# A 64-byte strip in front of the two split-weight buffers of a two-block fp32 transformer kernel

## The chip, the cores and the metric

The kernel runs on one core of one Trainium2 chip. The metric is the device time of one execution in microseconds. Below, the time before is the median of three runs; one more execution was taken by the hardware profiler, and every duration in the text comes from that one.

## The reference, cut to what matters

Two transformer blocks in fp32 on 256 tokens of width 2048. The first has an adaptive modulation, a wide input projection, stick-breaking and sparse attention, an output projection and a gated feed-forward network with a short convolution. The second block is run twice (two layers) with an input projection, small latent projections, three kinds of attention and an output projection. What fills the time are the products of a 256-token activation with a weight matrix from HBM:

```python
proj = h @ w_in[l]                       # 2048 x 5456
x = x + g1 * (merged @ w_out[l])         # 2048 x 2048
u = h @ w_up                             # 2048 x 11008
... @ w_down                             # 5504 x 2048
proj = jnp.einsum('bsd,dn->bsn', h, w_in[l])      # 2048 x 6726, twice
x = x + jnp.einsum('bsm,md->bsd', mixed, w_out[l])  # 2048 x 2048, twice
```

## The kernel before, in words

**Split products.** Each fp32 operand of a large product is split in two: a high part rounded to the type `fp32r` (which TensorE takes in one pass), and a low part, the rest. A product is three terms: high by high, low by high, high by low. The activation's parts are `HH` and `HLO` (line 109: 16 blocks of 128 rows by 256 tokens, each block 1024 bytes per partition), the weight's parts are `WHI` and `WLO` (line 116: four slots of 1024 columns each, 4096 bytes per partition).

**The stream of weights.** SyncE loads raw fp32 weights from HBM into `RAWT` (line 115, four slots of 2048 columns). For every half slot ScalarE writes the high part to `WHI` (`hi`, line 294), VectorE subtracts and writes the low part to `WLO` (`lo`, line 302), and TensorE runs the three terms (`three_terms`, lines 311 and 312, and `up_pe`, lines 1405, 1406 and 1410). Semaphores tie them: ScalarE may overwrite a slot when TensorE is past the product four half slots back, VectorE waits for ScalarE, TensorE waits for both. The order is written by hand.

**Two forms of matmul.** In the *row form* (line 312) an activation block of 128 tokens is loaded into the array as the stationary operand, and the weights stream through as the moving operand: 512 columns in the output projections and the down projection, 512, 496, 448, 416, 388 or 386 in the input projections. The moving operand then lies in `WHI` or `WLO`. In the *column form* (line 311, and 1405, 1406, 1410 for the up projection) 128 weight columns are stationary and the activation streams, 256 tokens: the moving operand lies in `HH` or `HLO`, the stationary in `WHI` or `WLO`. The latent products of block two take the activation from `LATHI` and `LATLO` (lines 110 to 112, names for places inside `BIG`) in either form; there the row form has 384 columns. Lines 877 to 879 are the row form at the end of an output projection, and 388 and 413 the modulation's share, interleaved with block one.

**Where things lie.** `sb` (line 103) asks for buffers one after the other, and the allocator puts them in that order, each start rounded up to 32 bytes. Per partition:

- `X`, `HH`, `HLO` and `BIG` start on multiples of 128 bytes (even multiples of 64).
- `BIG` has 13452 columns, 53808 bytes, which is 420 times 128 and 48 bytes more. `RAWT` therefore starts 64 bytes past a multiple of 128, an odd multiple of 64.
- `RAWT`, `WHI`, `WLO`, `AD`, `WK` and `KX` are multiples of 128 bytes long, so `WHI`, `WLO`, `AD`, `WK`, `KX` and `CST` all start on odd multiples of 64 too. `PV`, `MODC`, `BADA` and `SM` follow behind.
- `LATHI` starts 12608 bytes into `BIG` and `LATLO` 39488: both odd multiples of 64.

Inside a slot of `WHI` the two blocks of rows lie one behind the other (line 535: `o = (q % HL) * GR + k * n`, and the same in the other products), so with 512, 448 or 416 columns (2048, 1792, 1664 bytes) both blocks start with the parity of the buffer. With 496 columns (1984 bytes, an odd multiple of 64) the two blocks have opposite parity.

Of the kernel before, what the change touches and what calls it, by code (L numbers as in the profile page):

```python
# [93 lines left out]
def build_program(nc, x, c, positions, w_ada, b_ada, norm1_g, w_in, sb_norm_g, dsa_norm_g, w_out, norm2_g,  # L94
# [7 lines left out]
    with ctx:  # L102
        def sb(name, cols, dt=F32):
            return ctx.enter_context(nc.sbuf_tensor(name, [P, cols], dt))
# [8 lines left out]
            pass  # L113
        BIG = sb("BIG", 2 * W2)
        RAWT = sb("RAWT", RAW * 2 * GR)
        WHI, WLO = sb("WHI", HL * GR, F32R), sb("WLO", HL * GR, F32R)
        AD = sb("AD", 5 * 1024)
        WK = sb("WK", 3072)
# [159 lines left out]
        def raw_slot(gs):  # L278
            return RAWT[:, (gs % RAW) * 2 * GR:(gs % RAW + 1) * 2 * GR]

# [2383 lines left out]
```

How the kernel before makes its waits and increments, by code:

```python
        def ge(eng, sem, v):  # L172
            if isinstance(v, int) and v <= 0:
                return
            eng.wait_ge(sem, v)
# [7 lines left out]
            def __call__(self, ins):  # L184
                self.n += 1
                ins.then_inc(self.sem, 1)
                self.eng.wait_ge(self.sem, self.n)
# [99 lines left out]
        def hi(act, gs, reg, per_slot, j, size):  # L287
            q = 2 * gs + j
            if j == 0:
                act.wait_ge(raw_in[gs % RAW], reg * per_slot + uses[gs])
            ge(act, S("mm_done"), reg * 2 + (q - 3))
            r = raw_slot(gs)[:, j * size:(j + 1) * size]
            act.activation(WHI[:, (q % HL) * GR:(q % HL) * GR + size], r, ACT.Copy).then_inc(S("hi_done"), 1)
# [1 line left out]
        def lo(dve, gs, reg, j, size):  # L296
            q = 2 * gs + j
            dve.wait_ge(S("hi_done"), reg * 2 + (q + 1))
            r = raw_slot(gs)[:, j * size:(j + 1) * size]
            h = WHI[:, (q % HL) * GR:(q % HL) * GR + size]
            dve.tensor_tensor(WLO[:, (q % HL) * GR:(q % HL) * GR + size], r, h.bitcast(F32), ALU.subtract)\
               .then_inc(S("lo_done"), 1)
# [1 line left out]
        def three_terms(pe, parts, hi_at, lo_at, first, last):  # L305
# [6 lines left out]
                    pe.matmul(o, feat, weight, start=start, stop=stop)  # L312
            pe.wait_ge(S("hi_done"), hi_at)
            seen = set()
# [2 lines left out]
                seen.add(part[0])  # L318
                term(part, 1)
            pe.wait_ge(S("lo_done"), lo_at)
            left = [part[0] for part in parts]
```

## Time and profile before

| | |
|---|---|
| median of 3 runs | 2121.39 us (2120.06 to 2126.27) |
| the profiled execution's own time | 2119.28 us |
| its span, first to last instruction | 2117.4 us |
| granted TensorE clock, mean over the span | 0.987 |
| TensorE busy | 97% of the span, 13976 matmuls |
| VectorE, ScalarE, GpSimd busy | 66%, 48%, 6% |
| HBM read | 458.62 MB |

A busy row of TensorE counts a matmul from its start to its modelled end. Matmuls overlap in the pipeline, so a record is longer than the distance between two starts. That distance is called the pitch below.

### The profile page before, as it was taken

To read this page: it belongs to the slowest core of one execution; us is meant where nothing else is said; L and a number is where in the kernel's file an instruction comes from. 1 tells how busy PE (TensorE), PEld (TensorE's weight loads), DVE (VectorE), ACT (ScalarE), POOL (GpSimd) and SP (SyncE) were. 2 spreads that over 40 slices of the span, in tenths; PEclk is the share of its full clock that TensorE was granted. 3 is DMA by queue.
4 is the path that set the end of the run, shared out by engine and by line. 5 is a ranking of instruction groups with operands and counts; after the bars stand their busy time and mean duration, and the time that the engine had idled before them with its cause. 6 is when DMAs were issued, how large, how long until landed. Compare 5 with 4: busy or idle time off the path is not lost.

```text
span 2117.4 us, 33915 instructions
## 1 busy us (share of the span) xinstructions
PE 2055.6 (97%) x13976; PEld 1863.1 (88%) x13976; DVE 1404.7 (66%) x2153; ACT 1008.2 (48%) x1490; POOL 130.1 (6%) x113
## 2 busy tenths in 40 slices
PE   4999999998999999999999999999999999999997
PEld 1678998787999999998888899999988999999986
DVE  2358999886767667666567576556666756566665
ACT  2234445634554444454545455444564544445653
POOL 0000000012000000000011021000010110000100
PEclk6999999999999999999999999999999999999999
DMA  9998799593777777656655546545555556445553
GB/s 361 382 356 312 240 385 331 204 345 124 246 243 243 233 235 240 195 173 240 191 177 200 183 155 188 202 149 161 162 191 184 164 160 219 161 157 163 178 194 119
DMA packets 267317, 462.97 MB, mean 219 GB/s; under 512 B 21526, under 2 KB 160028, under 8 KB 266652
## 3 DMA queue, kind: packets, MB, share of 16 engines
q1 hardware_dynamic: 265832, 459.66, 64.2%
q8 instruction: 111, 1.82, 0.4%
q10 hardware_dynamic: 1332, 1.14, 0.2%
q14 instruction: 42, 0.34, 0.0%
HBM read 458.62 MB, written 2.13 MB: 218 GB/s over the span
## 4 chain that ended last, share of the span: by engine, by line
PE 86%; DVE 6%; DMA 3%; issue 2%; ACT 2%; ACTq 1%; POOL 0%; SPq 0%; DVEq 0%
PE PS L312 37%; PE PS L311 20%; PE PS L1405 7%; PE PS L1410 7%; PE PS L1406 7%; DVE WLO L302 2%; PE PS L1248 2%; DMA BIG<-w_ada 1%; ACT WHI L294 1%; PE PS L413 1%; DMA X<-x 1%; PE PS L1262 1%; DVE WK L1087 1%; DVE BIG L1733 1%; PE PS L1077 0%
## 5 line engine op out<-in xcount | busy, mean ns | idle before, releaser
L302 DVE TENSOR_TENSOR WLO<-RAWT,WHI 128x1024 fp32r<-128x1024 f32 (+7 forms) x694 | 829.8, 1202 | 401.0 <-ACT WHI L294 400.0
L294 ACT ACTIVATE WHI<-RAWT 128x1024 fp32r<-128x1024 f32 (+7 forms) x694 | 694.1, 1015 | 359.9 <-PE PS L1410 195.4
L312 PE MATMUL PS<-WHI,HH 128*128 128x512 f32 (+5 forms) x1296 | 503.3, 388 | 7.1 <-POOL HLO L1096 3.2
L312 PE MATMUL PS<-WHI,HLO 128*128 128x512 f32 (+5 forms) x1296 | 494.5, 382 | 0.0
L312 PE MATMUL PS<-WLO,HH 128*128 128x512 f32 (+5 forms) x1296 | 337.5, 382 | 1.3 <-DVE WLO L302 1.3
L1405 PE MATMUL PS<-HH,WHI 128*128 128x256 f32 x1376 | 327.1, 279 | 5.9 <-POOL HLO L1096 5.9
L1406 PE MATMUL PS<-HLO,WHI 128*128 128x256 f32 x1376 | 326.1, 278 | 0.0
L311 PE MATMUL PS<-HH,WHI 128*128 128x256 f32 x1280 | 312.0, 285 | 0.0
L311 PE MATMUL PS<-HLO,WHI 128*128 128x256 f32 x1280 | 303.2, 278 | 0.0
L312 PEld LDWEIGHTS PS<-WHI,HH 128*128 128x128 f32 x1296 | 244.4, 189 | 54.1 <-issue 7.2
L312 PEld LDWEIGHTS PS<-WLO,HH 128*128 128x128 f32 x1296 | 243.5, 189 | 43.1 <-DVE WLO L302 2.0
L312 PEld LDWEIGHTS PS<-WHI,HLO 128*128 128x128 f32 x1296 | 244.7, 189 | 39.1 <-issue 0.2
L1405 PEld LDWEIGHTS PS<-HH,WHI 128*128 128x128 f32 x1376 | 259.3, 188 | 7.3 <-POOL HLO L1096 7.3
L1406 PEld LDWEIGHTS PS<-HLO,WHI 128*128 128x128 f32 x1376 | 259.6, 189 | 0.0
L311 PEld LDWEIGHTS PS<-HH,WHI 128*128 128x128 f32 x1280 | 241.2, 188 | 6.4 <-issue 6.0
L311 PEld LDWEIGHTS PS<-HLO,WHI 128*128 128x128 f32 x1280 | 241.3, 189 | 0.4
L1410 PE MATMUL PS<-HH,WLO 128*128 128x256 f32 x1376 | 188.1, 279 | 0.0
L311 PE MATMUL PS<-HH,WLO 128*128 128x256 f32 x1280 | 174.4, 279 | 1.6 <-DVE WLO L302 1.6
L1410 PEld LDWEIGHTS PS<-HH,WLO 128*128 128x128 f32 x1376 | 172.1, 189 | 0.0
L311 PEld LDWEIGHTS PS<-HH,WLO 128*128 128x128 f32 x1280 | 159.2, 188 | 2.3 <-DVE WLO L302 2.2
L388 DVE SCALAR_TENSOR_TENSOR AD<-AD,SM 128x1024 f32<-128x1024 f32 x75 | 96.9, 1292 | 4.2 <-DMA AD<-w_ada 3.5
L814 ACT ACTIVATE HH<-BIG 128x256 fp32r<-128x256 f32 x102 | 42.1, 414 | 107.4 <-PE PS L312 106.7
(309 smaller groups left out, 1627.7 us busy)
## 6 DMA issues: line engine op xcount, KB each, us to landing
RAWT<-w_in SPq DMA_DIRECT2D x96, 1024.0 KB, 5.2
RAWT<-w_up SPq DMA_DIRECT2D x168, 512.0 KB, 4.9
AD<-w_ada SPq DMA_DIRECT2D x152, 512.0 KB, 6.3
RAWT<-w_out SPq DMA_DIRECT2D x96, 512.0 KB, 4.8
RAWT<-w_down SPq DMA_DIRECT2D x86, 512.0 KB, 4.6
BIG<-w_ada SPq DMA_DIRECT2D x40, 512.0 KB, 12.1
RAWT<-w_in SPq DMA_DIRECT2D x16, 832.0 KB, 4.6
RAWT<-w_in SPq DMA_DIRECT2D x16, 512.0 KB, 4.3
```

What stands on the lines that cost most here:

```text
L294: act.activation(WHI[:, (q % HL) * GR:(q % HL) * GR + size], r, ACT.Copy).then_inc(S("hi_done"), 1)
L302: dve.tensor_tensor(WLO[:, (q % HL) * GR:(q % HL) * GR + size], r, h.bitcast(F32), ALU.subtract)\
L311: return pe.matmul(o, weight, feat, start=start, stop=stop) if stationary else \
L312: pe.matmul(o, feat, weight, start=start, stop=stop)
L388: dve.scalar_tensor_tensor(acc, w, CS[:, kt:kt + 1], acc, ALU.mult, ALU.add)\
L413: mm = pe.matmul(PS[32 * j:32 * j + 32, 7, 0:T], col, w[:, j * T:(j + 1) * T], start=False, stop=kt == KT - 1)
L814: eng.activation(HHv[:, r, :], src(kt), ACT.Copy).then_inc(S("st_hi"), 1)
L1087: op = eng.tensor_scalar(f[:, j * T:(j + 1) * T], pb[:, j * T:(j + 1) * T], scale(kt), None if bias is None else bias(kt), ALU.mult, ALU.b ...
L1248: mm = eng.matmul(blk(scores(both[k], m + k), hf), l, r, start=z == 0, stop=z == len(prs[0]) - 1)
L1405: pe.matmul(o, WHI[:, wt[k, t]], HHv[:, kt, :], start=kt == 0 and t % 2 == 0, stop=False)
L1406: pe.matmul(o, WHI[:, wt[k, t]], HLv[:, kt, :], start=False, stop=False)
L1410: mm = pe.matmul(ffn_tile(par, t), WLO[:, wt[k, t]], HHv[:, kt, :], start=False, stop=kt == KT - 1 and t % 2 == 1)
```

## The change

An unused buffer of 16 fp32 columns, 64 bytes per partition, is allocated between `RAWT` and `WHI`. No instruction is added, removed or moved. `X`, `HH`, `HLO`, `BIG` (with `LATHI` and `LATLO`) and `RAWT` stay where they are; every buffer behind moves up by 64 bytes, so that `WHI`, `WLO`, `AD`, `WK`, `KX` and `CST` start on multiples of 128 bytes. `PV`, `MODC`, `BADA` and `SM` move as well.

```diff
         BIG = sb("BIG", 2 * W2)
         RAWT = sb("RAWT", RAW * 2 * GR)
+        sb("SHIFT", 16)
         WHI, WLO = sb("WHI", HL * GR, F32R), sb("WLO", HL * GR, F32R)
         AD = sb("AD", 5 * 1024)
```

## Rows read from the trace of the kernel before

**Rows 1.** The page: span, TensorE's busy share, and the chain that ended last.

```profile
span 2117.4 us, 33915 instructions
PE 2055.6 (97%) x13976; PEld 1863.1 (88%) x13976; DVE 1404.7 (66%) x2153; ACT 1008.2 (48%) x1490; POOL 130.1 (6%) x113
...
PE 86%; DVE 6%; DMA 3%; issue 2%; ACT 2%; ACTq 1%; POOL 0%; SPq 0%; DVEq 0%
```

**Rows 2.** Waits of TensorE: waiter, what it waited for: total us, times, longest.

```profile
PE PS L413 <- DMA AD<-w_ada: 10.1, 6, 4.4
PE PS L413 <- DMA BIG<-w_ada: 9.8, 10, 2.8
...
PE PS L312 <- DVE WLO L302: 1.3, 2, 0.7
```

**Rows 3.** Steady stretches: bounds, length, PE busy (matmuls), clock, DMA share, GB/s.

```profile
520.00:700.00 180.00, 180.00 (x1591) 1.00 0.77 249
710.00:885.00 175.00, 175.00 (x1488) 1.00 0.72 231
...
985.00:1105.00 120.00, 120.00 (x526) 1.00 0.63 204
...
156.00:167.50 11.50, 11.50 (x59) 1.00 1.01 378
142.00:152.00 10.00, 10.00 (x46) 1.00 0.78 266
1233.00:1245.50 12.50, 12.50 (x68) 1.00 0.55 170
```

**Rows 4.** Groups by line and shape: count, busy us, mean ns, idle before.

```profile
L312 PE MATMUL PS<-WHI,HH 128*128 128x512 f32 x880 | 349.4, 397 | 3.8 <-DVE HLO L820 2.0 <-ACT WHI L294 1.2 <-issue 0.6
...
L1405 PE MATMUL PS<-HH,WHI 128*128 128x256 f32 x1376 | 327.1, 279 | 5.9 <-POOL HLO L1096 5.9
...
L311 PE MATMUL PS<-HH,WHI 128*128 128x256 f32 x1280 | 312.0, 285 | 0.0
...
L312 PE MATMUL PS<-WHI,HH 128*128 128x416 f32 x128 | 45.7, 357 | 0.0
L312 PE MATMUL PS<-WHI,HH 128*128 128x496 f32 x96 | 40.2, 419 | 3.2 <-POOL HLO L1096 3.2
L312 PE MATMUL PS<-WHI,HH 128*128 128x448 f32 x64 | 23.8, 372 | 0.0
...
L877 PE MATMUL PS<-WHI,HH 128*128 128x512 f32 x32 | 12.5, 390 | 0.0
...
L312 PE MATMUL PS<-WHI,LATHI 128*128 128x384 f32 x16 | 5.4, 335 | 0.0
```

**Rows 5.** Pieces of the chain that ended last: start us, us, what.

```profile
1297.12 8.62 PE PS L311 x72
1305.74 4.17 PE PS L312 x24
...
1335.70 2.75 PE PS L311 x24
...
1338.67 2.83 PE PS L311 x24
```

**Rows 6.** Groups on VectorE in 412 to 446, block one's output projection.

```profile
L302 DVE TENSOR_TENSOR WLO<-RAWT,WHI 128x1024 fp32r<-128x1024 f32 x12 | 16.5, 1372 | 0.0
L388 DVE SCALAR_TENSOR_TENSOR BIG<-AD,SM,BIG 128x1024 f32<-128x1024 f32 x6 | 7.7, 1276 | 0.0
L388 DVE SCALAR_TENSOR_TENSOR AD<-AD,SM 128x1024 f32<-128x1024 f32 x5 | 7.4, 1482 | 0.0
```

**Rows 7.** Busy times in the same stretch; the columns PE, PEld, DVE, ACT, POOL.

```profile
412.00:446.00 34.00, 34.00 (x156) 28.10 (x155) 32.92 (x33) 14.95 (x18) 7.05 (x4) 1.00 0.92 342
```

**Rows 8.** Groups in 985 to 1105, the down projection.

```profile
L302 DVE TENSOR_TENSOR WLO<-RAWT,WHI 128x1024 fp32r<-128x1024 f32 x45 | 56.2, 1249 | 20.4 <-ACT WHI L294 20.4
L294 ACT ACTIVATE WHI<-RAWT 128x1024 fp32r<-128x1024 f32 x46 | 48.0, 1044 | 0.0
...
L820 DVE TENSOR_TENSOR HLO<-BIG,HH 128x256 fp32r<-128x256 f32 x44 | 19.5, 443 | 22.3 <-ACT HH L814 22.3
```

## The prediction

> **What bounds the kernel now.** The page first: TensorE is busy for 97% of a span of 2117.4 us, and 86% of the chain that ended last is its matmuls [rows 1]. Then its waits: the longest totals are 10.1 and 9.8 us, for transfers of the modulation's weights, and for the low parts of the weights it waited 1.3 us [rows 2]. In the long stretches it has no gap at all, at a granted clock of 1.00, that is 2.4 GHz [rows 3]. So the time is the number of matmuls times their pitch, and a layout that changes the pitch changes the time.
>
> **The pitch, and how it comes out of a row.** A stretch of length L counts every record that touches it, so pitch = (L + one record) / count. The records last some 390 ns with 512 columns and 279 with 256 [rows 4]. Then [rows 3]:
>
> - Column form, moving `HH` (even start): (180000 + 279) / 1591 = 113.3 ns in one stretch and (175000 + 279) / 1488 = 117.8 ns in another, the same instructions. In cycles of 2.4 GHz that is 256 + 16 and 256 + 27: two modes, each of which lasts as long as a stretch does. Short pieces show the same two: 2.75 us for 24 is 114.6, 2.83 us is 117.9 [rows 5].
> - Row form, 512 columns, moving `WHI` (odd start): 120392 / 526 = 228.9 ns, 512 + 37 cycles. 448 columns: 11872 / 59 = 201 ns, 448 + 35. 416 columns: 12857 / 68 = 189 ns, 416 + 38.
> - Latent products, moving `LATHI` (odd start): 8.62 us for 72 is 119.7 ns, 256 + 31; moving `WHI` over a stationary `LATHI`: 4.17 us for 24 is 173.8 ns, 384 + 33 [rows 5].
>
> What is to be seen: the surplus over one cycle per column doesn't grow from 256 to 448 columns, so it is a toll per matmul. It is 31 to 38 wherever the moving operand starts on an odd multiple of 64 bytes, and 16 or 27 where it starts on an even one. At equal width (256) the odd start costs 119.7 against 113.3, that is 6.4 ns, about 16 cycles, as many as 64 bytes of fp32 columns. The stationary operand doesn't sort the rows: it is odd for `HH` by `WHI`, odd for `LATHI` by `WHI`, even for `WHI` by `HH`.
>
> **The change part by part.** No instruction comes or goes. Four things move.
>
> 1. *Moving operand in `WHI` or `WLO`, odd to even.* I take off the 6.4 ns seen at equal width. The 512-column group counts 880, with its two sister terms 2640 matmuls, and lines 877 to 879 add 3 x 32 = 96; 416 columns: 3 x 128 = 384; 384 columns: 3 x 16 = 48; 448: 3 x 64 = 192 [rows 4]. Not all of them pay. In block one's output projection, 412 to 446 standing for 306 to 480 us, VectorE is busy 32.9 of 34.0 us beside a gapless TensorE, with modulation work of 1276 and 1482 ns apiece between its splits [rows 6, 7]: if TensorE speeds up, `WLO` is late next. That is 576 matmuls, which I count at nothing. The 448-column products run at a DMA share of 1.01 and 378 GB/s [rows 3]: nothing either. The 496-column ones change which half is odd, not how many: nothing. There remain 2064 + 96 + 384 + 48 = 2592, times 6.4 = 16.6 us, rounded to 17. In the down projection the cover is ample: per 12 matmuls (2.75 us) VectorE needs 1249 + 443 ns and ScalarE 1044 plus a split of that size, DMA moves 204 GB/s [rows 3, 8]; with 2.67 us they still fit.
>    Ends: if the toll falls to the even group's 16 cycles, 512 columns go to 220.0 ns, 8.9 less, and the sum is 2592 x 8.9 = 23 us. If it falls to 27, 224.6, 4.3 less, 11 us.
> 2. *Stationary operand in `WHI` or `WLO`, odd to even, under a moving `HH`.* 3 x (1376 + 1280) = 7968 matmuls [rows 4]. No row shows this pair of starts. By the chain's pieces about 3,000 of them now run at 117.8, half of these in one stretch around 710 to 885. Why a stretch takes one mode isn't to be seen, so I leave the mix: nothing. Ends: all in the fast mode, 3000 x 4.4 = 13 us less; all in the slow mode, 5000 x 4.4 = 22 us more.
> 3. *What ScalarE writes and VectorE reads and writes.* 694 splits on either engine. VectorE takes 1249 ns with an odd `WLO` [rows 8]; there is no even counterpart of that shape, so I take no change. They hide behind 2.75 us of matmuls; a price shows only in 306 to 480 us, where 48 splits at 5% of 1372 ns would be 3 us either way [rows 6].
> 4. *Buffers behind (`AD`, `WK`, `CST`, `SM`).* The same instructions on addresses 64 bytes up, a few per cent of TensorE's time: nothing, ends within those of point 3.
>
> Sum: 17 us less. The profiled execution's span would be 2117.4 - 17 = 2100; its own time, 2119.3, is 2.1 below the median, 2121.4, from which I subtract: **2104 us**, 0.8% less. A measurement of this kernel can tell about 0.3%, 6 us, from no change.
>
> **A rule weighed against the rows.** The granted pitch of 512 moving columns is 228.9 ns, of 256 it is 113.3 to 117.8 [rows 3]. The Trainium skill ("TensorE: Matmul & The Clock Gate", Back-to-back issue gap) gives the gap of warm matmuls as N/2.4 plus some 2.5 ns, 216 ns at 512 columns, and knows no toll for a start address. If the shift took the whole toll away, its figure would give 2592 x 12.9 = 33 us less for point 1, 2088 us. No row here comes within 10 cycles of it, so it enters nothing.
>
> **The rivals.**
>
> *Nothing happens: the start isn't the cause.* `LATHI` differs from `HH` in more than parity (short products, other distance to `WHI`), and the toll of the row form may belong to a weight stream that two engines write meanwhile. For: the 496-column products, half of which start even already, have (10000 + 397) / 46 = 226 ns, 496 + 46, the highest toll of all [rows 3]. Against: the toll is 31 to 33 both with `LATHI` moving, which nobody writes then, and with `WHI` moving over it [rows 5]. Time: 2121, give or take 5. The Trainium skill sides with this rival ("SBUF — State Buffer", Specifications): lines of 16 bytes, of which either start is a whole multiple. The forecast coupled with all column-form matmuls in the slow mode (17 less, 22 more) ends here as well. Chance 0.18.
>
> *Slower: the loads collide with the streams.* The load of the next stationary operand starts with the current matmul, so two streams read at once. Now an even `HH` streams over an odd `WHI`; after the change both start even. The one column-form case of equal parity in the trace is `LATHI` by `WHI`, both odd, and it is the slowest, 119.7 [rows 5]. If equal parity is the cause, the 7968 column-form matmuls go from a mean of (4968 x 113.3 + 3000 x 117.8) / 7968 = 115.0 to 119.7: 37 us more. The row form would lose at most its surplus over 33 cycles, 1.7 ns x 2592 = 4 us. Time: 2121 + 33 = 2154. It decides from the point where the column form's mean pitch passes 115.0 + 17000 / 7968 = 117.1; there it has eaten the gain. Against: `WHI` over `HH` is unequal now and pays 35 to 38. Chance 0.14.
>
> *More than forecast.* The mode of 117.8 comes of the odd stationary start, and with it gone all run at 113.3, and the row form at 16 cycles of toll: 13 + 23 = 36 us less, 2085. For: every matmul with an even moving and an even stationary start is unseen. Chance 0.13.
>
> *The change doesn't do what it says.* The strip could end up elsewhere, or unallocated; the starts follow from the order and sizes of the buffers, and the strip keeps its place. Below 0.02, counted with the first rival.
>
> **How the numbers follow.** Forecast 0.55, by itself 2092 to 2116: the row form's 11 to 23, the mix some 5 either way. With nothing 0.18, slower 0.14, more 0.13. The range leaves out 0.06 below, where the third case is complete, and 0.12 above, most of the slower case: 2083 to 2128. Faster by over 0.3%: the forecast but for 0.02, and the third case, 0.66. Slower by over 0.3%: the slower case and 0.02 of the first: 0.16. Within 0.3%: 0.18.
>
> **What would show it.** In 985 to 1105 us the 512-column matmuls at 222.5 ns (some 541 in 120 us for 526) confirm point 1; 220.0 is the upper end, 228.9 the first rival. The column form in 520 to 885 us tells point 2: 113.3 or 117.8, and 119.7 or more is the slower rival. The latent products (72 in 8.62 us) should stay if the moving start alone counts. The 496-column ones should stay at 226. VectorE waited for by TensorE between 306 and 480 us shows the share I count at nothing. It is wrong if pitches fall that I don't name, or if the pitch falls as said and the time doesn't, through waits for `WLO`.

## The result, and the profile after

The changed kernel takes 2151.1 us in the median (2150.3 to 2151.9, 4 runs) beside 2121.8 us for the kernel before: ratio 1.0144, 95% interval 1.0128 to 1.0159. It is slower by 29 us (27 to 34 by the ratio's interval), where 17 us less, 2104 us, was forecast, and lies outside the range of 2083 to 2128. The rival "the loads collide with the streams" had 2154 us and a chance of 0.14.

The page of the changed kernel, against [rows 1]; its lines are numbered one higher from line 116 on:

```profile
span 2148.9 us, 33915 instructions
PE 2093.3 (97%) x13976; PEld 1892.2 (88%) x13976; DVE 1405.0 (65%) x2153; ACT 1009.7 (47%) x1490; POOL 129.9 (6%) x113
...
PE 88%; DVE 6%; issue 2%; ACT 2%; DMA 2%; ACTq 1%; POOL 0%; SPq 0%; DVEq 0%
```

The same 13976 matmuls keep TensorE busy for 37.7 us more (2093.3 against 2055.6), while the other engines' busy times stay within 1.5 us. TensorE's idle time falls by 6.2 us (span less busy: 55.6 against 61.8), and 37.7 - 6.2 is the span's 31.5. So TensorE doesn't wait more; the matmuls themselves are further apart.

Steady stretches, as in [rows 3] (bounds, length, PE busy and matmuls, clock, DMA share, GB/s):

```profile
520.00:700.00 180.00, 180.00 (x1502) 1.00 0.74 237
710.00:885.00 175.00, 175.00 (x1478) 1.00 0.72 231
...
1000.00:1120.00 120.00, 120.00 (x516) 1.00 0.63 204
156.00:167.50 11.50, 11.50 (x59) 1.00 0.99 383
142.00:152.00 10.00, 10.00 (x46) 1.00 0.98 358
```

By the prediction's formula the column form now has (180000 + 283) / 1502 = 120.0 and (175000 + 283) / 1478 = 118.6 ns where it had 113.3 and 117.8. The row form with 512 columns has (120000 + 395) / 516 = 233.3 where it had 228.9. Pieces of the chain, against [rows 5]:

```profile
1316.40 8.18 PE PS L312 x72
1324.58 4.16 PE PS L313 x24
```

The latent products, whose moving operand did not move, went the other way: 8.18 us for 72 is 113.6 ns, before 119.7. That is the line that decides against "the moving start counts alone".

In the down projection the splits take what they took [rows 8]:

```profile
L303 DVE TENSOR_TENSOR WLO<-RAWT,WHI 128x1024 fp32r<-128x1024 f32 x44 | 53.9, 1225 | 20.6 <-ACT WHI L295 20.6
...
L295 ACT ACTIVATE WHI<-RAWT 128x1024 fp32r<-128x1024 f32 x45 | 47.0, 1044 | 0.0
```

Taken over the whole trace from the distances between starts, with the gaps of waits left out, the column form's mean rises from 115.3 to 119.0 ns (7770 distances: 29 us), the 512-column row form's from 229.1 to 232.8 (2660: 10 us), the latent column form's falls from 119.7 to 114.9 (214: 1 us). That is 38 us, against the 37.7 that the page shows. Of the other widths, 448 columns rise from 200.6 to 203.7 ns, and 416 stay (188.1 and 188.4).

### The profile page after: what moved, and what is told of

Read it like the earlier page. It is cut to its first block, busy times and chain, and to the rows that moved or that the text cites. A ratio compares the mean times of both kernels' runs of the same rounds, so it can differ in the third digit from the quotient of the medians.

```text
span 2148.9 us, 33915 instructions
## 1 busy us (share of the span) xinstructions
PE 2093.3 (97%) x13976; PEld 1892.2 (88%) x13976; DVE 1405.0 (65%) x2153; ACT 1009.7 (47%) x1490; POOL 129.9 (6%) x113
## 4 chain that ended last, share of the span: by engine, by line
PE 88%; DVE 6%; issue 2%; ACT 2%; DMA 2%; ACTq 1%; POOL 0%; SPq 0%; DVEq 0%
PE PS L313 38%; PE PS L312 20%; PE PS L1406 7%; PE PS L1411 7%; PE PS L1407 7%; DVE WLO L303 2%; PE PS L1249 2%; PE PS L414 1%; ACT WHI L295 1%; DMA X<-x 1%; PE PS L1263 1%; DVE WK L1088 1%; DVE BIG L1734 1%; DMA BIG<-w_ada 1%; PE PS L1078 0%
## 5 line engine op out<-in xcount | busy, mean ns | idle before, releaser
L1406 PE MATMUL PS<-HH,WHI 128*128 128x256 f32 x1376 | 338.3, 284 | 4.7 <-POOL HLO L1097 4.7
L1407 PE MATMUL PS<-HLO,WHI 128*128 128x256 f32 x1376 | 337.1, 283 | 0.0
L312 PE MATMUL PS<-HH,WHI 128*128 128x256 f32 x1280 | 319.5, 288 | 0.0
L312 PE MATMUL PS<-HLO,WHI 128*128 128x256 f32 x1280 | 311.2, 282 | 0.0
L1411 PE MATMUL PS<-HH,WLO 128*128 128x256 f32 x1376 | 193.0, 282 | 0.0
L312 PE MATMUL PS<-HH,WLO 128*128 128x256 f32 x1280 | 178.2, 282 | 0.2 <-DVE WLO L303 0.2
L1411 PEld LDWEIGHTS PS<-HH,WLO 128*128 128x128 f32 x1376 | 176.3, 189 | 0.0
L312 PEld LDWEIGHTS PS<-HH,WLO 128*128 128x128 f32 x1280 | 163.0, 188 | 0.4 <-DVE WLO L303 0.4
```

The source lines that it names most:

```text
L312: return pe.matmul(o, weight, feat, start=start, stop=stop) if stationary else \
L1406: pe.matmul(o, WHI[:, wt[k, t]], HHv[:, kt, :], start=kt == 0 and t % 2 == 0, stop=False)
L1407: pe.matmul(o, WHI[:, wt[k, t]], HLv[:, kt, :], start=False, stop=False)
L1411: mm = pe.matmul(ffn_tile(par, t), WLO[:, wt[k, t]], HHv[:, kt, :], start=False, stop=kt == KT - 1 and t % 2 == 1)
```

## The experiments

Two theories were tested one after the other. The first, which the expectations of the first four experiments (e1 to e4) state, was equal parity: a matmul is slow when both operands start on odd, or both on even, multiples of 64 bytes. e1 refuted it, and from e5 on the theory is that the distance between the places of the two operands counts. Call D the start of `WHI` less the start of the activation's buffer, modulo 256 bytes. It is 64 for `HH` and 0 for `LATHI` before the change, 128 and 64 after it. (`HH` and `HLO`, `WHI` and `WLO`, and the blocks inside them lie multiples of 256 bytes apart, but for products of 496, 416, 388 or 386 columns. At 416 the two blocks have D = 64 and 192 before and 128 and 0 after, at 448 both have 64 and then 128.) Pitches below are means of start distances in steady stretches. In the stretches looked at, a steady column form on a given D takes one of at most two values.

**Where does the strip have to stand?** Four kernels, each the kernel before with one edit:

```diff
 e1_strip128:     RAWT = sb("RAWT", RAW * 2 * GR)
+        sb("SHIFT", 32)
 e2_all_moved:    X = sb("X", 2 * D)
+        sb("SHIFT", 16)
 e3_behind_wlo:   WHI, WLO = sb("WHI", HL * GR, F32R), sb("WLO", HL * GR, F32R)
+        sb("SHIFT", 16)
 e4_between:      WHI = sb("WHI", HL * GR, F32R)
+        sb("SHIFT", 16)
+        WLO = sb("WLO", HL * GR, F32R)
```

> Strip of 128 bytes in front of WHI instead of 64: WHI and WLO are odd again, HH stays even. Theory (equal parity of the moving and the stationary start, as an odd or even multiple of 64 bytes, makes the load collide with the stream): parities are unequal again, so the time returns to that of before, 2121 us within 6, the column form to 113.3 or 117.8 ns, LATHI by WHI back to 119.7. Rival (the distance counts in more than its parity, or any move away from the old place hurts): a time of its own, 2130 or more, or a pitch that neither kernel has.

2144.3 us, ratio 1.0105 (1.008 to 1.013). Parity is refuted as the rule: `WHI` is odd again and the time does not come back. Stretches of this kernel, with the columns of [rows 3]: the column form runs at 117.8 in nearly every stretch (113.3 in two short ones), the row form at 233.3, and the latent products (D now 128) at 118.6:

```profile
520.00:690.00 170.00, 170.00 (x1446) 1.00 0.76 246
720.00:885.00 165.00, 165.00 (x1403) 1.00 0.71 232
1015.00:1105.00 90.00, 90.00 (x388) 1.00 0.61 191
```

(170283 / 1446 = 117.8, 165283 / 1403 = 117.8, 90396 / 388 = 233.0; one record more or less in the count is 0.6 ns, and the start distances themselves give 233.3.) The rival "more than its parity" stands.

> The 64-byte strip stands in front of HH, so HH, HLO, BIG, RAWT, WHI and WLO all move by 64 bytes: WHI and WLO are even as in the changed kernel, but HH is odd, so that the parities are unequal. Theory (equal parity collides): 2121 us within 6. Rival (an even start of WHI and WLO is itself the cause, by its own streams or by what ScalarE and VectorE write there): 2151 us.

2116.3 us, ratio 0.998 (0.9963 to 0.9996). `WHI` lies as in the changed kernel, and the cost is gone. The place of the weights by itself doesn't matter; the column form has 113.3 and 117.8 again, the row form 228.9, and `LATHI`, moved along, 119.7.

> The strip stands behind WLO: WHI and WLO stay, and only AD, WK, KX, CST and the small buffers behind move by 64 bytes. Theory (equal parity of HH and WHI): 2121 us within 6. Rival (the 29 us come from the other buffers that the change moved, AD, WK and CST): up to 2151 us.

2119.0 us, ratio 0.9983 (0.9965 to 1.000). The buffers behind cost nothing.

> The strip stands between WHI and WLO: WHI stays odd, WLO is even. One of three terms, high by low, has equal parity with HH. Theory (it is a matter of the two starts of one matmul and its neighbour): about a third of the 29 us, 2128 to 2134 us, with the pitch of the WLO term raised alone or with a neighbour of it. Rival (both weight buffers must be even, or VectorE's reading and writing of unequal starts matters): 2121 or 2151 us.

2124.1 us, ratio 1.001 (0.9995 to 1.0025), less than the 2128 to 2134 expected. The pitches rise by about their third in the row form (229.1 to 230.6) but by only a sixth in the column form (115.3 to 115.9 against 119.0). Its steady stretches, with the columns of [rows 3]:

```profile
520.00:690.00 170.00, 170.00 (x1473) 1.00 0.75 243
720.00:885.00 165.00, 165.00 (x1431) 1.00 0.73 236
```

That is 115.6 and 115.5 ns, and (2 x 113.3 + 120.0) / 3 is 115.5. So the thirds come out if the two unmoved terms take the fast mode everywhere, also in 720 to 885 us, where the kernel before ran at 117.8. Why they take it with the third term at another distance isn't shown. The time moves less than the pitches: TensorE's busy time is 8.5 us above before (2064.1 against 2055.6), the profiled span only 2.8 (2120.2 against 2117.4), as its idle time falls.

**How does the cost go with the distance?** Buffers that exist anyway serve as strips, as there is too little room for empty ones; `MODC` and `BADA` no longer stand at their old place where they appear here:

```diff
 e5_strip32:      RAWT = ...
+        sb("SHIFT", 8)
 e6_384_64:       RAWT = ...
+        MODC = sb("MODC", 96)
+        sb("SHIFT", 16)
 e7_768:          RAWT = ...
+        MODC = sb("MODC", 96)
+        BADA = sb("BADA", 96)
 e8_384_96:       RAWT = ...
+        MODC = sb("MODC", 96)
+        sb("SHIFT", 24)
```

> Strip of 32 bytes in front of WHI. What counts is taken to be the distance from HH to WHI and WLO; 64 bytes more cost 29 us, 128 bytes more 23 us. Theory (the distance modulo 256 bytes, in steps of 64): a start inside a step behaves as a mixture, 2121 to 2151 us, with a column-form pitch between 115.3 and 119.0 ns. Rival (any start off a multiple of 64 bytes costs one more access per stream): slower than both, over 2155 us.

2149.4 us, 1.0119 (1.0059 to 1.0178). D is 96: column form 117.3 or 118.7, row form 233.4. Inside the theory's range, but at its upper end, and the row form is above both neighbours, so steps of 64 bytes are too coarse a picture. The rival's 2155 us or more isn't reached.

> MODC (384 bytes) and a strip of 64 bytes stand in front of WHI, so the distance from HH grows by 448 bytes. Modulo 256 it is then a whole multiple, the case of LATHI by WHI in the kernel before (119.7 ns in the column form, 173.6 ns for 384 columns in the row form). Theory (distance modulo 256 bytes): column form at 119.7 to 120, row form near 229 ns, so 4.5 x 7770 = 35 us more, 2150 to 2158 us. Rival (parity modulo 128 bytes, with a detail that the 128-byte strip upset): as the changed kernel, column form 119.0 and row form 232.8 ns. Rival (only the distance modulo 512 or more counts): pitches not seen yet.

2146.6 us, 1.0115 (1.0087 to 1.0144). D is 0 for `HH`, and its column form is now at 120.0 everywhere, the value that `LATHI` had. The latent products, at 192, take 113.5 (8.17 us for 72). The row form falls to 227.3, below before, which makes the total 3 us less than the least I expected.

> MODC and BADA (768 bytes together) stand in front of WHI: the distance from HH grows by three times 256 bytes. Theory (distance modulo 256 bytes): as before, 2121 us within 6, column form at 113.3 or 117.8 ns, row form 229.1, LATHI by WHI 119.7. Rival (modulo 512 bytes or a larger power of two): 768 is half of 512 away from a multiple, so pitches and time differ from before, by 10 us or more.

2119.9 us, 0.9991 (0.9964 to 1.0018). Three times 256 bytes change no pitch. This settles the period of 256 bytes against 512 and larger powers of two; e1 had excluded 128.

> MODC (384 bytes) and a strip of 96 bytes in front of WHI: the distance from HH is 32 bytes past a multiple of 256, half a step below that of the kernel before. Theory (distance modulo 256): column form between that of a whole multiple (119.7) and that of before (115.3), 2121 to 2156 us. Rival (half a step suits the load and the stream better): column form at 113.3 throughout, some 15 us below before, 2106 us.

2150.8 us, 1.0128 (1.0068 to 1.0188). D is 32: column form 118.3, row form 233.3. Half way between the two places is no better place.

> The 64-byte strip stands in front of RAWT, so RAWT moves along with WHI and WLO; HH, HLO and BIG stay. Theory (distance from HH to WHI): as the changed kernel, 2151 us within 6, with column form 119.0 and row form 232.8 ns. Rival (the distance from RAWT to WHI and WLO, over which ScalarE and VectorE split the weights): 2121 us.

```diff
         BIG = sb("BIG", 2 * W2)
+        sb("SHIFT", 16)
         RAWT = sb("RAWT", RAW * 2 * GR)
```

2148.9 us, 1.0131 (1.0103 to 1.0159), column form 118.7, row form 232.8: the changed kernel again, with `RAWT` moving along. So the distance from `RAWT` to `WHI` and `WLO`, over which the weights are split, isn't the cause.

> All as in the kernel before, but LATHI and LATLO lie 64 bytes further into BIG, so that their distance to WHI leaves the whole multiple of 256 bytes. Theory: the latent products in the column form go from 119.7 to 113.3 ns, 432 matmuls, 2.6 us less in all, 2116 to 2119 us; everything else keeps its pitch. Rival (the short products are slow for another reason): 119.7 ns and the time of before.

```diff
-LATENT, KVB = (3152, 9872), W2 - 1536
+LATENT, KVB = (3168, 9888), W2 - 1536
```

Pieces of the chain of waits in this kernel, as in [rows 5]:

```profile
1296.50 8.16 PE PS L311 x72
1304.67 4.19 PE PS L312 x24
```

2118.9 us, 0.9994 (0.9981 to 1.0008): too small for the timing, but plain in the pitch. D of the latent products is 192 instead of 0, and 72 take 8.16 us instead of 8.62, with nothing else moved.

**The cost by itself.**

```python
def col(i, d):
    k, t = i % 8, i // 2 % 8
    return PS[:, k % 4, 0:T], WHI[:, d // 4 + t * P:d // 4 + (t + 1) * P], HH[:, k * T:(k + 1) * T]
...
for i in range(96): pe.matmul(*col(i, 64), start=True, stop=True)
```

> The disputed cost by itself. This kernel leaves out the whole computation: it loads one stretch of weights, makes an HH and a WHI of them, and then runs nothing but blocks of 96 matmuls, each block at another distance from HH to WHI (0 to 320 bytes in the column form, 0 to 256 in the row form), with the other engines idle. Its output is a copy of a piece of input. Theory (the load of the next stationary operand and the stream of the moving one collide by their distance modulo 256 bytes): the same pitches as in the full kernels, column form 120 ns at 0 and 256, 113.3 or 117.8 at 64, 192 and 320, 118.7 to 120 at 128; row form lower at 0 and 64 (227, 229) than at 128 and 192 (233). Rival (the collision is with what ScalarE, VectorE or the transfers write): one pitch at all distances.

Groups by line of this kernel, one block of 96 matmuls each: the row form at D = 0, then the column form at D = 128, 256, 160, 192, 64 and 320 (count, busy us of the block, mean ns of a record):

```profile
L169 PE MATMUL PS<-WHI,HH 128*128 128x512 f32 x96 | 22.0, 390 | 0.0
...
L157 PE MATMUL PS<-HH,WHI 128*128 128x256 f32 x96 | 11.8, 286 | 0.0
L165 PE MATMUL PS<-HH,WHI 128*128 128x256 f32 x96 | 11.8, 284 | 0.0
L159 PE MATMUL PS<-HH,WHI 128*128 128x256 f32 x96 | 11.8, 283 | 0.0
...
L161 PE MATMUL PS<-HH,WHI 128*128 128x256 f32 x96 | 11.6, 280 | 0.0
L153 PE MATMUL PS<-HH,WHI 128*128 128x256 f32 x96 | 11.6, 282 | 0.0
...
L167 PE MATMUL PS<-HH,WHI 128*128 128x256 f32 x96 | 11.1, 277 | 0.0
```

A block's busy time is 95 distances, the first ones longer, and one record. The steady values, beside those of the full kernels:

| D, bytes | column form alone | in full kernels | row form, 512, alone | in full kernels |
|---|---|---|---|---|
| 0 | 120.0 | 120.0 (e6) | 226.7 | 226.7, mean of all 227.3 (e6) |
| 32 | 118.3 | 118.3 (e8) | 233.3 | 233.3 (e8) |
| 64 | 117.8 or 113.3 | 117.8 or 113.3 (before) | 228.9 | 228.9 (before) |
| 96 | 117.3 | 117.3 or 118.7 (e5) | 233.3 | 233.4 (e5) |
| 128 | 120.0 | 118.7 or 120.0 (after) | 232.4 | 232.4 or 233.3 (after) |
| 160 | 120.0 | | 234.2 | |
| 192 | 117.8 | 117.8, seldom 113.3 (e1) | 233.3 | 233.3 (e1) |
| 224 | 116.7 | 116.7 (e8, latent) | 233.3 | |

With ScalarE, VectorE and GpSimd idle and a DMA share of 0.01, most pitches of the full kernels come back to a tenth of a nanosecond; a few that the full kernels show beside them (118.7 at 96 and 128, 233.3 at 128, 113.3 at 192) do not. The rival that another engine's writes are the other party falls. Two more blocks of the column form, at 16 and 48 bytes, took 118.3 and 117.8. Blocks at 256 and 320 behave as at 0 and 64, save that 64 took 117.8 and 320 took 113.3. In m1 `HH` stays and only the place read in `WHI` moves, so that it is the distance and not the place rests on e2, where both moved and no pitch changed, and on f2 below, where only the activation moved. Which of the two a run takes was my open point 2.

**What sets the mode.**

> The two modes of the column form by themselves. As the kernel of the distances, the computation is left out and the other engines are idle; blocks of 48 column-form matmuls at a distance of 64 bytes (four at the end at 192) follow different short separators: 1, 2, 3, 4 or 16 matmuls of 2 columns, 1, 2 or 4 of 128, some of the row form, some narrower ones. The first eight kinds come twice, the second time in another place. Theory (the mode is set by the phase in which a run of matmuls begins, and then holds): within a block one pitch, 113.3 or 117.8 ns, and the same kind of separator gives the same mode both times or nearly so. Rival (the mode depends on the other engines or drifts by itself): changes within a block, or no relation to the separator.

Timeline of that kernel (start us, us, line, operands, count); the blocks of 48 stand between separators:

```profile
31.82 0.50 PE L143 MATMUL PS<-CST 128*128 128x2 f32 x4
32.19 5.71 PE L147 MATMUL PS<-HH,WHI 128*128 128x256 f32 x48
37.73 0.50 PE L143 MATMUL PS<-CST 128*128 128x2 f32 x4
38.09 5.90 PE L149 MATMUL PS<-HH,WHI 128*128 128x256 f32 x48
43.83 0.73 PE L143 MATMUL PS<-CST 128*128 128x2 f32 x6
44.42 5.71 PE L151 MATMUL PS<-HH,WHI 128*128 128x256 f32 x48
49.97 0.95 PE L143 MATMUL PS<-CST 128*128 128x2 f32 x8
50.77 5.90 PE L153 MATMUL PS<-HH,WHI 128*128 128x256 f32 x48
...
67.28 0.39 PE L156 MATMUL PS<-CST 128*128 128x128 f32 x2
67.42 5.70 PE L157 MATMUL PS<-HH,WHI 128*128 128x256 f32 x48
...
156.50 5.71 PE L187 MATMUL PS<-HH,WHI 128*128 128x256 f32 x48
162.05 0.95 PE L143 MATMUL PS<-CST 128*128 128x2 f32 x8
162.85 5.90 PE L189 MATMUL PS<-HH,WHI 128*128 128x256 f32 x48
```

(An fp32 matmul leaves two records.) After 3 matmuls of 2 columns the block takes 5.71 us, that is 113.3 ns, both times; after 4, 5.90 us, 117.8, both times. After 1, 2 or 4 matmuls of 128 fp32 columns all six blocks are fast. Within a block the pitch settles in the first six matmuls and never changes, but for the stretches at half the clock told of below. So within the order of this kernel the mode came back with the separator and belongs to how the run began. The separator alone doesn't decide it: the first block took the fast mode behind 2 matmuls of 2 columns that followed the fp32 matmuls at the kernel's start, while behind 2 such matmuls after another block the mode was the slow one, both times. What ran before the separator counts too. The distance does as well: four blocks at D = 192 were slow behind 1, 2, 3 and 16, and at D = 64 the block behind 3 was fast.

**Does it hold in the full kernel, and can it be used?**

```diff
 f1_dummy:
                         ada_reduce(pe, ada[0])
+                        pe.matmul(PS[:, 6, 0:P], ident, ident, start=True, stop=True)
 ...
 f2_row0, in kout (and the two splits of out2_start alike):
+                ro = r * T if order else r * T + 16
 ...
-                        eng.activation(HHv[:, r, :], src(kt), ACT.Copy).then_inc(S("st_hi"), 1)
+                        eng.activation(HH[:, ro:ro + T], src(kt), ACT.Copy).then_inc(S("st_hi"), 1)
 ...
 f3_all: both, and LATENT = (3168, 9888)
```

> The kernel before, with one matmul of 128 fp32 columns, unused, behind the modulation's sum inside the up projection, since in the kernel of the modes every run that followed a 128-column fp32 matmul took the fast mode. Theory (a run's mode is set by the phase of its start, and this restart sets it): the stretch of 1536 matmuls that began at 706.7 us and ran at 117.8 ns runs at 113.3: 1536 x 4.4 = 6.8 us less, less some 0.2 us for each of the added matmuls, 2112 to 2114 us; the stretch behind it stays fast. Rival (in the full kernel other things set the mode): the mix stays or turns without a relation, 2119 us or more.

Timeline of TensorE in this kernel around the start of the stretch:

```profile
704.33 1.84 PE L397 MATMUL PS<-CST,AD 128*128 128x2 f32 x16
706.03 0.47 PE L1417 MATMUL PS<-CST 128*128 128x128 f32 x2
```

The stretch behind it, with the columns of [rows 3]:

```profile
720.00:885.00 165.00, 165.00 (x1458) 1.00 0.74 237
```

2113.8 us, ratio 0.9975 (0.9962 to 0.9987). The line runs twice, at 706.0 and 882.2 us. Behind the modulation's sum (line 397) and the first unused matmul the stretch that ran at 117.8 now has 165278 / 1458 = 113.4 ns. The theory's 6.6 us less are 5.3 in the ratio, within its interval.

> The kernel before, with the activation's slots of the down projection and of the last two output projections moved by 64 bytes inside HH and HLO, so that the row form there has a distance of a whole multiple of 256 bytes between WHI and HH, while the column form keeps 64 bytes. Theory (distance modulo 256 bytes, and the row form's best place is 0): the 512-column pitch there falls from 228.9 to 226.7 ns, 86 x 12 + 2 x 32 x 12 = 1800 matmuls times 2.2 = 4.0 us less, 2115 us. Rival (the activation's place doesn't matter): 228.9 ns and 2119 us.

2114.8 us, ratio 0.9978 (0.9969 to 0.9988), 4.7 us less; (90000 + 390) / 399 = 226.5 ns in the down projection, a stretch with the columns of [rows 3]:

```profile
1015.00:1105.00 90.00, 90.00 (x399) 1.00 0.56 178
```

Moving the activation by 64 bytes does what moving the weights the other way does, for the form where D = 0 is best, while the column form keeps D = 64. The range of the ratio excludes the rival's 2119 us.

> The unused matmul, the row form's slots and the latent parts moved by 64 bytes together. If the three are independent: 6.5 + 4.0 + 2.6 = 13 us less than before, 2106 us, faster than both kernels. If the modes are redrawn by the other two edits, some of it is lost or gained, by up to 6 us.

2110.3 us, ratio 0.9963 (0.9947 to 0.9978) against the kernel before: faster than both kernels, by 8 us and 41 us. All three pitches are there (column 114.4 in the mean, row 227.8 over all stages, latent 114.8), TensorE's busy time is 2044.4 us, 11.2 below before, and the profiled span 2107.3, 10.1 below. The median shows less than the 13 expected; its interval reaches from 5 to 11 us, so at least 2 us of the 13 are missing, and which of the three gives less in the time isn't shown.

## Why the prediction was wrong, point by point

**What bounds the kernel** was right: TensorE doesn't wait more, and the pitch makes the time. Reading the pitch from rows was right too, to 0.1 ns.

**The step that failed** is in the reading of the pitches: "The stationary operand doesn't sort the rows", and from it point 1 of the change, a toll of 6.4 ns taken off 2592 matmuls. I sorted the five rows by the parity of the moving start, and then by that of the stationary start, each by itself. Their difference I tried only as equal or unequal, modulo 128 bytes. The rows carried the answer's other half: [rows 3, 5] hold D = 64 for `HH` and D = 0 for `LATHI`, and 119.7 was the pitch of D = 0, not of an odd start. The surplus of 31 to 38 cycles in the row form isn't the toll of an odd moving start either; at every distance tried the row form pays 32 to 50 cycles, 544 to 562 for 512 columns.

**Point 1**, row form, 17 us less: it became 3.7 ns more on the 2660 distances between 512-column matmuls, 10 us more. The 448-column products, counted at nothing for their DMA share, got 3.1 ns slower too (0.6 us on 192 matmuls). **Point 2**, column form, counted at nothing with ends of -13 and +22 us: it became 29 us more, outside both ends, since D = 128 has other values (118.7 and 120.0) than either known mode. The rival that had 120 for it came closest; I gave it 0.14 because the row form seemed to speak against equal parity. Its time was met within 3 us, partly by luck: its column form was 37 us up and its row form 4 down, where 29 up and 10 up were measured and 6 us of idle time fell away, and its rule is refuted by e1. **Points 3 and 4**, the splits and the other buffers, at nothing: right (1225 and 1249 ns; e3, e9). **The 576 matmuls of block one's output projection at nothing**: the changed kernel slows them as well (229.0 to 232.4 ns between 306 and 481 us); VectorE, busy nearly all the time there, could only have taken away a gain. **The 496-column products**: unchanged, 226 ns as said, though for no reason that I had.

**The rules.** The Trainium skill ("SBUF — State Buffer", Specifications) has lines of 16 bytes. Either start is a whole multiple of these, and still 64 bytes are worth 29 us here, so the multiple of 16 bytes doesn't tell where a buffer costs time. The Trainium skill ("TensorE: Matmul & The Clock Gate", Step-by-step) also says that loading the next tile's weights doesn't steal read bandwidth from the running matmul. That is hard to square with m1, which has nothing but the loads, the moving streams and the results written to PSUM, and where the pitch goes from 113.3 to 120.0 ns with the place of one operand against the other. The gap of 216 ns for 512 columns that the Trainium skill ("TensorE: Matmul & The Clock Gate", Back-to-back issue gap) gives for a single matmul was reached at no distance at the full clock; the least here, with a load for every matmul, was 226.7.

**What is shown and what is inferred.** Shown, for these shapes: of all the places moved here only the distance of the two operands modulo 256 bytes changed the pitch, no other engine has to take part, and which of two modes a run takes goes back to its start. That the two reads meet in the same part of memory, and push each other until they have a rhythm that avoids or repeats the meeting, fits all of it and is not shown. Which phase leads to which mode isn't known beyond the separators tried, nor why D = 128 has 118.7 in some stretches and 120.0 in others.

## What to carry to other kernels

In a kernel bound by back-to-back fp32r matmuls, an unrelated buffer can change the time by over a per cent through the distance between weights and activations modulo 256 bytes. Fix it by hand, measure the few distances in a kernel of matmuls alone, and re-measure after each change of the allocation. The column form and the row form want different distances (64 and 0 here), and the activation's slots can be moved as well as the weights. Where rows have two operands each, sort them by the difference of the places before sorting by either.

## What the runs showed of the hardware that was not expected

A run of equal matmuls took one of two pitches, 272 or 282.7 cycles of 2.4 GHz for 256 columns at D = 64, and held it for 1536 matmuls. A few short matmuls ahead of it, with what ran before them, decide which.

At half the clock the column form had no toll at D = 64 and 192. In two of the three blocks of m2 behind 16 matmuls of 2 columns the granted clock fell to 0.50, and ten records lie in 1.5 us (last columns: clock, DMA share, GB/s):

```profile
57.00:60.00 3.00, 3.00 (x29) 1.00 0.00 0
60.90:62.40 1.50, 1.50 (x10) 0.53 0.00 0
64.50:67.00 2.50, 2.50 (x23) 1.00 0.02 7
218.00:219.50 1.50, 1.50 (x10) 0.50 0.00 0
```

The steady distance there is 213.3 ns, 256 cycles of 1.2 GHz, against 282.7 cycles of 2.4 GHz in the same block a microsecond later. The row form wasn't seen at that clock.
